# Shorter router steps in both layers, and first-layer experts placed by 7 x rank modulo 30

## The reference, cut to what matters

```
p1 = softmax(tokens @ w1 + b1)              # 4 groups, the best one is taken
lg2 = (tokens @ w2 + b2)[the group's 8]     # 32 experts, 8 in a group
top_val, top_idx = top_k(lg2, 2)
gate = p_grp * softmax(top_val)             # two weights a token
y[token] += gate * (silu(x @ w_gate[e]) * (x @ w_up[e])) @ w_down[e]    # for its two experts e
```

## Time and profile before

| | |
|---|---|
| median of 3 runs | 2017.17 us |
| profiled execution: time / span | 2015.87 / 2014.0 us |
| PE busy | 1789.0 us (89%) |
| DVE busy | 1017.2 us (51%) |
| POOL / ACT busy | 566.7 / 418.1 us |
| HBM read | 572.08 MB, 285 GB/s over the span |
| chain that ended last | PE 62%, DMA 26%, DVE 6% |

### The profile page before, as it was taken

How to read it: one execution, slowest core, us unless ns; L and a number is a source line. 1 busy time by engine, 2 the same in 40 slices (tenths; PEclk the granted TensorE clock), 3 DMA queues, 4 the chain that set the end, 5 groups by cost and what they waited for, 6 DMA issues and landing times.

```text
span 2014.0 us, 56742 instructions
## 1 busy us (share of the span) xinstructions
PE 1789.0 (89%) x23884; PEld 1238.6 (61%) x23885; DVE 1017.2 (51%) x2416; ACT 418.1 (21%) x832; POOL 566.7 (28%) x431
## 2 busy tenths in 40 slices
PE   7999989999999987898988967667669989999998
PEld 4444466666666654645776745445447777788887
DVE  3798156677666656346345633333246995210001
ACT  2001242212211214115341211111113224210001
POOL 0000026777766761001033522222248000100000
PEclk9999989999999998999989987887888889999999
DMA  9854168899999999822169999999996255433320
GB/s 369 310 205 167 42 233 351 340 422 429 427 430 429 427 430 396 294 84 74 43 249 429 417 428 428 429 428 429 429 413 236 101 217 202 167 126 126 126 105 21
DMA packets 109379, 574.33 MB, mean 285 GB/s; under 512 B 4976, under 2 KB 10224, under 8 KB 84592
## 3 DMA queue, kind: packets, MB, share of 16 engines
q1 hardware_dynamic: 108720, 570.72, 70.7%
q10 hardware_dynamic: 576, 2.43, 0.3%
HBM read 572.08 MB, written 1.05 MB: 285 GB/s over the span
## 4 chain that ended last, share of the span: by engine, by line
PE 62%; DMA 26%; DVE 6%; issue 2%; ACT 2%; SPq 2%; DVEq 0%; ACTq 0%
PE bank L349 24%; PE bank L554 14%; DMA ring<-in_expert_w_gate 11%; DMA ring<-in_expert_w_down 7%; DMA ring<-in_expert_w_up 6%; PE bank L526 4%; PE bank L974 4%; PE bank L508 3%; PE bank L601 3%; DVE b L1034 2%; ACT b L1847 2%; DMA ring<-in_conv_w_in 1%; PE bank L890 1%; PE bank L420 1%; DMA ring<-in_attn_w_in 1%
## 5 line engine op out<-in xcount | busy, mean ns | idle before, releaser
L554 PE MATMUL bank<-ring,b 128*32 128x128 f32 (+1 forms) x13600 | 521.0, 310 | 133.7 <-DMA ring<-in_expert_w_gate 75.3
L554 PEld LDWEIGHTS bank<-ring,b 128*32 128x32 f32 x13600 | 402.3, 116 | 305.4 <-issue 155.1
L1034 DVE TENSOR_TENSOR h_t<-h_t,bank 128x512 f32<-128x512 f32 (+1 forms) x696 | 349.9, 564 | 316.6 <-PE bank L526 316.6
L349 PE MATMUL bank<-h_t,ring 128*128 128x256 f32 (+1 forms) x1600 | 424.0, 427 | 5.2 <-ACT h_t L1847 2.5
L1847 ACT ACTIVATE b<-bank 128x256 f32<-128x256 f32 (+4 forms) x371 | 142.8, 400 | 1298.0 <-PE bank L554 749.5
L349 PEld LDWEIGHTS bank<-h_t,ring 128*128 128x128 f32 x1600 | 306.9, 193 | 116.5 <-issue 77.4
L2269 POOL TENSOR_SCALAR b<-b 128x1024 f32<-128x1024 f32 (+1 forms) x85 | 195.1, 2295 | 46.0 <-POOL b L2277 33.6
L2277 POOL TENSOR_TENSOR b<-b 128x512 f32<-128x512 f32 (+1 forms) x85 | 88.8, 1045 | 411.5 <-PE bank L526 411.5
L526 PE MATMUL bank<-b 32*128 32x512 f32 (+1 forms) x1392 | 172.3, 565 | 5.4 <-DVE h_t L1034 4.7
L1034 DVE TENSOR_TENSOR b<-b,bank 128x128 f32<-128x128 f32 (+3 forms) x124 | 49.9, 406 | 234.4 <-PE bank L349 155.0
L2272 POOL TENSOR_TENSOR b<-b,b 128x1024 f32<-128x1024 f32 (+1 forms) x85 | 161.6, 1901 | 7.1
(11 more groups left out here) (298 smaller groups left out, 1464.0 us busy)
## 6 DMA issues: line engine op xcount, KB each, us to landing
ring<-in_expert_w_gate SPq DMA_DIRECT2D x64, 2048.0 KB, 18.7
ring<-in_expert_w_up SPq DMA_DIRECT2D x64, 2048.0 KB, 21.2
ring<-in_expert_w_down SPq DMA_DIRECT2D x64, 2048.0 KB, 21.5
ring<-in_ada_w SPq DMA_DIRECT2D x24, 2048.0 KB, 15.1
ring<-in_w_mod SPq DMA_DIRECT2D x12, 2048.0 KB, 9.1
ring<-in_w_in SPq DMA_DIRECT2D x6, 2048.0 KB, 10.5
ring<-in_w_ffn_gate SPq DMA_DIRECT2D x5, 2048.0 KB, 7.8
ring<-in_w_ffn_up SPq DMA_DIRECT2D x5, 2048.0 KB, 8.2
```

Of the source, the lines that this page charges most:

```text
L349: last = pe.matmul(o, lhs(k), rhs(k), start=(k == 0), stop=(k == nk - 1))
L554: last = pe.matmul(b[32 * m:32 * m + 32, 0:width], lhs[:, k, :], rhs[:, k, m * width:(m + 1) * width], start=(k == 0), stop=(k == nk - 1), ...
L1034: return dv.tensor_tensor(o, a, b, op)
```

## The change

- `ranks`: the all-ones products of one tile go to all later tiles and the total at once (right side broadcast), and the triangle of tiles 1 and up is one product: 6 products where there were 14 in layer 0, 4 where there were 5 in layer 1; the counts by expert (4 products, layer 0) stay.
- Layer 0: pieces 14 and 15 stand between the h transposes, after the third and the sixth group; pieces 12 to 15 are turned after the ranks; piece 16 stands behind the order product in place of piece 15 before it; piece 17 is behind the bases.
- Layer 1: only piece 24 stands before the logits, 25 and 26 behind the transposes, 27 at the end.
- `place` is 7 x rank + 1, less 30 for each full round, for ranks 2 and up; ranks 0 and 1 keep their places. `by_rank` and `first_two` are set up once, as is a 4-column mask in `ones_m`.
- The broadcast: the eight small values now lie so that one PE transpose of `small` puts the four wanted ones at rows 0, 32, 64 and 96 on; ACT copies them four times (twice in layer 1), scaled by the mask, into `value_rows`; four products with 32 rows each spread them. PE waits for `placed` and makes the transpose before `dispatch(0)`. POOL's four products go.

```diff
-ROUTER0 = (range(12, 14), range(14, 15), range(15, 18))
-ROUTER1 = (range(24, 26), (), range(26, 28))
+ROUTER0 = ((12, 13), (14, 15), (16, 17))
+ROUTER1 = ((24,), (25, 26), (27,))
...
+                for i in range(2 * tiles):
+                    t, half = i // 2, i % 2
+                    group("a", lambda b: transposes(b, [
+                        (P * kk, H[:, 4 * half + kk, t * P:(t + 1) * P]) for kk in range(4)]))
+                    if layer == 0 and i in (2, 5):
+                        piece(pieces[1][i // 3])
...
                 def ranks(b):
-                    for t in range(tiles + 1):
-                        for s in range(min(t + 1, tiles)):
-                            tri = cn("before") if s == t else ones_c[:, :]
-                            last = pe.matmul(b[:, NE * t:NE * t + NE], tri, sel[:, s, :],
-                                             start=(s == 0), stop=(s == min(t, tiles - 1)))
+                    pe.matmul(b[:, 0:NE], cn("before"), sel[:, 0, :], start=True, stop=True)
+                    for s in range(tiles):
+                        later = tiles - s
+                        last = pe.matmul(v3(b, NE * (s + 1), later, NE), ones_c[:, :],
+                                         sel[:, s:s + 1, :].broadcast_to([P, later, NE]),
+                                         start=(s == 0), stop=(s == tiles - 1))
+                        if s == 0:
+                            pe.matmul(v3(b, NE, tiles - 1, NE), cn("before"), sel[:, 1:tiles, :], start=False, stop=False)
...
-                for p in pieces[1]:
+                for p in pieces[1] if layer else pieces[0] + pieces[1]:
                     turn_piece(p)
                 if layer == 0:
-                    piece(pieces[2][0])
                     pe.wait_ge(sem("order_ready"), 1)
                     group("v", lambda b: pe.matmul(b[:, 0:NE + 1], n_chunks[0:NE, NE:NE + 1].broadcast_to([NE, P]),
                                                    later[0:NE, :], start=True, stop=True))
+                    piece(pieces[2][0])
                     pe.wait_ge(sem("order_ready"), 2)
...
+                pe.wait_ge(sem(f"placed{layer}"), 1)
+                group("a", lambda b: transposes(b, [(0, small)]))
                 dispatch(0)
+                pe.wait_ge(a_free, lane["a"])
+                rows = value_rows.rearrange("p t n -> p (t n)")
                 for i in range(4):
-                    pe.wait_ge(sem(f"diag_ready{layer}"), i + 1)
-                    group("a", lambda b: pe.matmul(b[:, 0:ntok], ones_c[:, :], diag[i][:, 0:ntok], start=True, stop=True))
+                    group("a", lambda b: pe.matmul(b[:, 0:ntok], ones_c[32 * i:32 * i + 32, :], rows[32 * i:32 * i + 32, 0:ntok],
+                                                   start=True, stop=True, tile_position=(32 * i, 0)))
...
-                    step(dv.tensor_scalar(place_end, expert_rank, -2.0, 2.0 * NE, ALU.mult, ALU.add))
-                    do(dv.tensor_scalar(place, expert_rank, 2.0, -1.0, ALU.mult, ALU.add))
-                    do(dv.tensor_scalar(place, place, place_end, 0.0, ALU.min, ALU.max))
+                    step(dv.tensor_scalar(place, expert_rank, 7.0, 1.0, ALU.mult, ALU.add))
+                    do(dv.tensor_scalar(rounds, expert_rank, 7.0 / 30, -1.0 / 30 + 1.0 / 60 - 0.5, ALU.mult, ALU.add))
+                    do(dv.tensor_scalar(rounds, rounds, ROUND, ROUND, ALU.add, ALU.subtract))
+                    do(dv.scalar_tensor_tensor(place, rounds, -30.0, place, ALU.mult, ALU.add))
+                    do(dv.tensor_scalar(place, place, by_rank, first_two, ALU.mult, ALU.add))
...
+                b = full()
+                for t in range(tiles):
+                    ins = act(value_rows[:, t, :], b[:, 0:P], ACT.Copy, scale=ones_m[:, t:t + 1])
+                taken(ins)
...
-                po.wait_ge(sem(f"placed{layer}"), 1)
-                g = [small[:, 4 * i:4 * i + tiles] for i in (0, 1, 6, 5)]
-                for i in range(4):
-                    po.tensor_tensor(v3(diag[i], 0, tiles, P), ident.unsqueeze(1).broadcast_to([P, tiles, P]),
-                                     g[i].unsqueeze(2).broadcast_to([P, tiles, P]), ALU.mult) \
-                        .then_inc(sem(f"diag_ready{layer}"), 1)
```

More of the change, by code:

```diff
@@ L245, in two_blocks @@
         picks, caps = v3(b3, 3456, 2, 4), v3(b3, 3464, 2, 4)
[L246 removed]
+        value_rows = v3(b12, 6656, 4, P)
         route, logit_t = v3(b3, 4640, 4, 36), b3[:, 4784:5040]
@@ L251, in two_blocks @@
         small = b3[:, 5648:5776]
+        value_at = (0, 32, 20, 24, 28, 96, 64, 52)
         slot_id, lane = b3[:, 5812:5813], sm[:, 26:27]
@@ L255, in two_blocks @@
         order = sm[:, 30:63]
-        expert_rank, place, place_end, base = [b3[:, 3872 + i:3873 + i] for i in range(4)]
+        by_rank, first_two = sm[:, 29:30], sm[:, 63:64]
+        expert_rank, place, rounds, base = [b3[:, 3872 + i:3873 + i] for i in range(4)]
         q_tok, kv_tok, kd_t = v3(b12, 0, 2, 512), v3(b12, 1024, 4, 256), v3(b12, 2048, 4, TOK)
@@ L448, in moe @@
                 group("v", lambda b: transposes(b, [(P * c, logit_t[:, c * P:(c + 1) * P]) for c in range(tiles // 2)]))
[L449 to L454, removed]
-                for p in pieces[1]:
-                    piece(p)
+                for i in range(2 * tiles):
[4 more added lines that the diff above has]
+                        piece(pieces[1][i // 3])
                 if layer == 1:
+                    for p in pieces[0]:
+                        turn_piece(p)
+                    for p in pieces[1]:
+                        piece(p)
                     for j in range(2):
@@ L1118, in moe @@
                 l1, l2 = route[:, 0:tiles, 0:NG], route[:, 0:tiles, NG:36]
-                g = [small[:, 4 * i:4 * i + tiles].unsqueeze(2) for i in range(8)]
-                four = [v3(small, 32 + 16 * i, 4, NG)[:, 0:tiles, :] for i in range(4)]
+                g = [small[:, at:at + tiles].unsqueeze(2) for at in value_at]
+                four = [v3(small, 4 + 32 * i, 4, NG)[:, 0:tiles, :] for i in range(4)]
                 to4 = lambda a: a.broadcast_to([P, tiles, NG])
@@ L1353, in _ @@
             do(tt(order[:, NE:NE + 1], order[:, NE:NE + 1], lane, ALU.subtract))
+            step(dv.tensor_scalar(by_rank, lane, 2.0, None, ALU.is_ge))
+            step(dv.scalar_tensor_tensor(first_two, lane, 2.0, lane, ALU.is_lt, ALU.mult))
             do(dv.tensor_scalar(order[:, NE:NE + 1], order[:, NE:NE + 1], float(NE), None, ALU.add))
@@ L1411, in _ @@
             fuse(0, 3, "ln1", 0)
+            do(tt(ones_m[:, 0:4], cn("iota", 0, 4), lane.broadcast_to([P, 4]), ALU.is_equal))
             dv.tensor_copy(st[:, 0:1], mods[:, 0:1]).then_inc(sem("mods_ready"), 1)
@@ L1930, in moe @@
                     taken(act(rows, b.rearrange("p (m q k) -> p m q k", m=2, k=KD), ACT.Copy))
+                    if layer == 0 and i in (2, 5):
+                        take_piece(pieces[1][i // 3])
                 ac.wait_ge(a_free, taken.n)
                 ac.sem_inc(copied.sem, 2 * tiles)
-                for p in pieces[0]:
-                    take_turned(p)
-                g = [small[:, 4 * i:4 * i + tiles] for i in range(8)]
-                four = [v3(small, 32 + 16 * i, 4, NG)[:, 0:tiles, :] for i in range(3)]
+                if layer == 1:
+                    for p in pieces[0]:
+                        take_turned(p)
+                g = [small[:, at:at + tiles] for at in value_at]
+                four = [v3(small, 4 + 32 * i, 4, NG)[:, 0:tiles, :] for i in range(3)]
                 ac.wait_ge(sem(f"router_shift{layer}"), 1)
@@ L1940, in moe @@
                 act(g[5], g[4], ACT.Exp).then_inc(sem(f"router_exp{layer}"), 1)
-                for p in pieces[1]:
-                    take_piece(p)
                 if layer == 1:
+                    for p in pieces[1]:
+                        take_piece(p)
                     for j in range(4):
```

## The result

The changed kernel takes 1995.95 us (median of 4 runs, 1995.08 to 1998.44) against 2016.88 (4 runs, 2014.78 to 2017.70): a ratio of 0.9899, 95% interval 0.9886 to 0.9912, so 1.0% faster. 1999 was forecast, with 1991 to 2009 as its range. Measured twice more beside other kernels it gave 0.9925 and 0.9900; about half of what lies between these is the part of the outcome that the prediction did not have.

A forecast was written before the change was run, and what follows sets the result against it. DMA, full in both expert stages, was taken to bound the kernel. Router 0's 7 us, the order's 6 and router 1's 5 summed to 18, giving 1999 us with the median 1.3 over the profiled run; range 1991 to 2009.

The forecast's parts named there:

- What bounds the kernel: Both expert stages: DMA is full there, so a stage ends earlier if its DMA starts earlier or has fewer holes.
- The order: First layer's expert loop: new places cut DMA holes from 10.8 to 4.8 us, stage ends 6 us earlier; bounds 3 and 11.
- Both holes: First expert loop: two DMA holes of about 2.4 us remain, at places 15 and 22, near 530 and 635.
- The recurrence: Model of expert loops: 9.36 us a chunk, 4.89 a load, ring of two experts, two fitted lags; gives holes and stage end.
- Router 1: Second layer's router: moved pieces and cheaper broadcasts bring weight loads and loop start forward, 5 us earlier; bounds 3 and 6.
- Router 0: First layer's router: first expert matmul at 298, 7 us earlier, and the loop's first load with it; bounds 4 and 9.
- one low-clock stretch: Router 0: a modulation piece takes 1.95 us at full clock, 3.31 at low; one low stretch assumed, first expert matmul at 298.
- the price of the broadcast: Router 0: four products on separate row groups replace 8 records in 3.70 us, taking 1.14; saves 2.6 us.
- The holes did not merely move: Rival on the first loop's order: holes only move, leaving 7 + 5 us gained, 2005 us; chance 0.12.
- The router gains were not lost: Rival on the routers: their gains are lost, the order's stays, 6 + 1 us left, 2010 us; chance 0.09.
- no slowdown: Rival on the first expert loop: TensorE's clock falls in DMA waits, 14 uncovered low stretches cost 19.6 us, 2019 us; chance 0.06.

The follow-up runs named there:

- order alone: The kernel before with only the new places of the experts, its routers left old: 2008.44 us, ratio 0.9965.
- the other offset: The changed kernel with rank r at place 2 + (7r + 8) mod 30, so a three-chunk expert stands last: 2011.83 us, ratio 0.9978.
- falling order: The changed kernel with layer 0's experts placed by rank, two-chunk experts together and one-chunk ones behind them: 2056.26 us, one run.
- the second measurement: The changed kernel itself once more, unchanged, beside versions with its parts taken back: 2002.02 us, ratio 0.9925.

## Why the prediction was right, and where it was off

*What bounds the kernel* held. In ten profiles with the new order router 0 is between 39.4 and 47.0 us long, and the loop behind it is 450.0 to 451.3 in every one: what the first load gains is still there at the loop's end. From there to piece 24 the same ten spread from 246.1 to 248.6, where no part of the change lies.

*The order*: 6 forecast, 7.0 measured in the full change, 6.1 in order alone. Both holes came where named, near 530 and 635, at 2.1 us each for 2.4. 11.2 less 4.2 is the 7.0. The last down product was forecast near 760 and started at 759.68. The recurrence also gave 17 (16.3) and 63 (61) us for two orders it was not fitted to.

*Router 1*: 5 forecast, 5.3 measured. Up1 was forecast near 1033 and the loop near 1042, on the old time scale. Less the 12.2 us by which piece 24 came earlier, this is 1020.8 and 1029.8; it was 1020.93 and 1029.97. The term is nearly all the moved pieces (4.5). That it goes through DMA, by up1, is argued from the traffic and was not tested apart from the loop start.

*Router 0*: 7 forecast with bounds 4 to 9, 3.3 measured, below the lower bound. This is the mis-sized term. The first expert matmul did come at 298.64 where 298 stood in the forecast, but 1.6 of that was the earlier logits, which I had not taken out. The right sum was 4.7 to the first expert matmul. It fell short because I took one low-clock stretch, and pieces 16 and 17 both ran in it (3.64 twice, where the low price was 3.31). In two other profiles with the same router, of the kernel with the other offset and of the one in falling order, piece 17 takes 1.95 and router 0 is 40.0 and 40.6 long, a gain of 6.8 and 6.3: so 7 was attainable; which one comes goes with where the low clock falls, and no run set that on purpose. Another 1.4 us went between the first expert matmul and the first load: the 1.02 us "issue" gap in the first up product, and the later combine. The forecast had 0.5 to 1 for this and did not carry it to the load. With it goes the price of the broadcast: the forecast counts 2.6 for it, and the run with the old broadcast shows 1.7 at the first expert matmul and 0.3 at the first load. The four products did shrink by 2.6 (3.70 to 1.14), but the transpose, the copies and the gaps took most of it back.

*What was missed* is the collision with the MEMSETs. I wrote that VectorE's arithmetic would come 4 us earlier and looked only at what TensorE had queued there; the same timeline of the kernel before has GpSimd's MEMSETs at 282.29 to 286.0, in the stretch that the arithmetic was to move into. With the collision router 0 gains nothing (46.96 against 46.85); the one measurement of the changed kernel whose profile shows it came to 2002. It was seen in full in two of the nine profiles in which counts and MEMSETs fall together, in part in two more.

The errors nearly cancel, and that is luck: order +1.0, router 1 +0.3, chance ahead of it +1.6, router 0 -3.7 make -0.8 of 18. The time was 3 us below the forecast because the profiled run, 1998.44, is the highest of its four, while I had added 1.3 for the median.

*Rivals.* The holes did not merely move (their sum is 4.2, not 11). The router gains were not lost, though in the second measurement router 0's were. The clock stayed at 1.00 in the first loop: no slowdown; the kernel in falling order shows that the mechanism exists (0.90), but with a wait at each expert, not once a pair.

*Open* is what decides whether VectorE gets in between two MEMSETs or only behind the last; the operations stand 0.2 us apart in both cases. Open too is the "issue" gap of 0.3 to 2.7 us in the first products of each loop, which varies between kernels with the same code there. Neither was tried by itself.

## What to carry to other kernels

When two resources are near balance, the order of the work decides: write the ring as a recurrence, fit its lags to the holes of the trace you have, and let it price an order before you run it. When a change moves a chain of small operations earlier, look at what every engine does in the stretch it moves into, GpSimd beside VectorE above all, and not only at the engine that gets its result. Measure a stage from its own start, or the clock's chance ahead of it is counted as gain; and of a difference of 6 us between two measurements of one kernel, part may have a cause that the trace shows (here 3.4).

## What the runs showed of the hardware

- A series of nine GpSimd MEMSETs (128x512 f32, 0.47 us each in the eight recorded together) held one 128x33 VectorE TENSOR_SCALAR for 4.04 us, in place of 0.18, up to the end of the ninth; in other profiles of the same code it took 0.34 or 0.79, which fits the end of the first or second MEMSET, and the eight took 3.97 or 3.93 for 3.75. Beside ScalarE clearing the same memory, with one MEMSET left, it took 0.33.
- Beside GpSimd's diagonal products of the old broadcast, a 128x256 TENSOR_TENSOR of VectorE's slot arithmetic took 1.00 us, where it takes 0.42 in the changed kernel without them, and the two 128x128 ones behind it 1.93 together for 0.37.
- Which modulation piece falls into the low clock changes from profile to profile of nearly the same router: the 64 matmuls of piece 17 took 3.64 us in the changed kernel and 1.95 in two kernels with another order of the experts (the other offset and the falling one), and router 0 was 3.5 and 3.0 shorter in those.
